# A hybrid state-space, attention and Hyena backbone: four reordered seams, and the carried part scaled on ScalarE

## The reference

```python
mod = silu(c) @ w_ada[l] + b_ada[l]; mod_c = silu(c_ctx) @ w_ada[l] + b_ada[l]
shift, scale, gate = jnp.split(mod[:, None, :], 3, axis=-1)
u = _layer_norm(h) * (1.0 + scale) + shift
uc = _layer_norm(hc) * (1.0 + scale_c) + shift_c
z, xbc, dtr, q, k, v, gd, hp, gh = jnp.split(u @ w_in, IN_SPLITS, axis=-1)

# state-space group: 4 groups of 4 heads of 64, state 128, chunks of 128 tokens, both directions
la = jnp.cumsum(dtc * a, axis=2)
y_diag = jnp.einsum('bclsgr,bcsgrp->bclgrp', w.astype(x.dtype), xc)
def step(h, inp):
    dec, st = inp
    return h * dec[..., None, None] + st, h
y_off = jnp.einsum('bclgn,bcgrpn->bclgrp', cc, h_start) * jnp.exp(la)[..., None]
y = y_f + flip(y_b) + dsk * xs
o_ssd = _rms_norm(y_ssd * silu(z)) * ssd_norm_w

# attention group: 4 heads, two score maps of 64 each
s = jnp.einsum('bqhmd,bkhmd->bhmqk', q, k) * DIFF_SCALE
p = softmax(s); attn = p[:, :, 0] - lam * p[:, :, 1]
o_diff = (_rms_norm(attn @ v) * (1.0 - lam_init)) * silu(gd)

# Hyena group: z = x1 * longconv(v); o_hy = x2 * longconv(z) * silu(gh), by FFT with implicit filters
h_new = _layer_norm(ALPHA * h + gate * (concat(o_ssd, o_diff, o_hy) @ w_out)) * ln_g + ln_b
```

## Time and profile before

| | us |
|---|---|
| median of 3 runs (lowest, highest) | 3764.7 (3757.56, 3769.51) |
| the profiled execution, its time | 3763.57 |
| its span in the trace | 3761.8 |
| granted TensorE clock, mean | 0.958 |
| busy: PE, DVE, ACT, POOL | 3348.2, 2404.3, 1104.9, 994.6 |
| state-space stages, about | 1487 to 1708 and 3335 to 3540 |
| norm stages, about | 4 to 91 and 2015 to 2103 |

### The profile page before, as it was taken

How to read it: one execution, slowest core, us unless ns; L and a number is a source line. 1 busy time by engine, 2 the same in 40 slices (tenths; PEclk the granted TensorE clock), 3 DMA queues, 4 the chain that set the end, 5 groups by cost and what they waited for, 6 DMA issues and landing times. The chain is left out here.

```text
span 3761.8 us, 47984 instructions
## 1 busy us (share of the span) xinstructions
PE 3348.2 (89%) x18164; PEld 2728.6 (73%) x18164; DVE 2404.3 (64%) x3965; ACT 1104.9 (29%) x2003; POOL 994.6 (26%) x790
## 2 busy tenths in 40 slices
PE   6999999999958887996997989999999588868798
PEld 2787888888848876665783677888888488845577
DVE  4134566765448996996665324556875489969755
ACT  3112222212335555332210311222221355523321
POOL 0033334342202222211220023433343022232111
PEclk9999999999979998998998999999999799989899
DMA  5354232223171331434426155322332633133441
GB/s 204 79 158 147 82 93 90 92 85 103 57 216 43 98 102 60 161 117 154 140 79 229 54 128 171 97 87 82 108 97 75 205 93 96 43 114 114 142 147 62
DMA packets 416681, 423.57 MB, mean 113 GB/s; under 512 B 57168, under 2 KB 353104, under 8 KB 415298
## 3 DMA queue, kind: packets, MB, share of 16 engines
q1 hardware_dynamic: 369316, 314.17, 28.8%
q10 hardware_dynamic: 47136, 106.32, 8.0%
HBM read 287.76 MB, written 124.01 MB: 109 GB/s over the span
## 5 line engine op out<-in xcount | busy, mean ns | idle before, releaser
L778 PE MATMUL l_p_acc<-l_u_hi,l_w_hi 128*128 128x512 f32 (+1 forms) x2208 | 606.0, 376 | 29.8 <-ACT l_p_stg L842 16.1
L778 PE MATMUL l_p_acc<-l_u_hi,l_w_lo 128*128 128x512 f32 (+1 forms) x2208 | 588.3, 368 | 0.0
L778 PE MATMUL l_p_acc<-l_u_lo,l_w_hi 128*128 128x512 f32 (+1 forms) x2208 | 587.1, 367 | 0.0
L778 PEld LDWEIGHTS l_p_acc<-l_u_hi,l_w_hi 128*128 128x128 f32 x2208 | 383.7, 189 | 106.8 <-issue 33.2
L693 POOL TENSOR_TENSOR l_w_hi<-l_wt,l_p_zero 128x1024 fp32r<-128x1024 f32 x100 | 199.3, 1993 | 925.1 <-PE l_p_acc L778 758.1
L778 PEld LDWEIGHTS l_p_acc<-l_u_hi,l_w_lo 128*128 128x128 f32 x2208 | 381.2, 189 | 71.9
L778 PEld LDWEIGHTS l_p_acc<-l_u_lo,l_w_hi 128*128 128x128 f32 x2208 | 381.3, 189 | 71.7
L1512 PE MATMUL l_at_pS<-l_at_k_hi,l_at_q 128*128 128x512 f32 (+1 forms) x400 | 166.0, 415 | 125.1 <-ACT l_at_prob L1628 68.9
L1753 DVE TENSOR_REDUCE l_at_nmax<-l_at_pS 128x1 f32<-128x1280 f32 (+1 forms) x144 | 197.4, 1371 | 121.0 <-PE l_at_pS L1513 119.1
L695 POOL TENSOR_TENSOR l_w_lo<-l_wt,l_w_hi 128x1024 fp32r<-128x1024 f32 x100 | 266.4, 2664 | 7.9
L935 DVE TENSOR_TENSOR l_p_R<-l_p_sw,l_p_rs 128x512 f32<-128x512 f32 x72 | 49.7, 690 | 286.4 <-PE l_p_sw L757 286.4
(11 more groups left out here) (362 smaller groups left out, 7193.2 us busy)
## 6 DMA issues: line engine op xcount, KB each, us to landing
l_wt<-w_in SPq DMA_DIRECT2D x104, 512.0 KB, 3.9
l_n_wa<-w_ada SPq DMA_DIRECT2D x10, 2048.0 KB, 17.0
kf_d<-l_p_R SPq DMA_DIRECT2D x72, 256.0 KB, 3.7
xbc_d<-l_p_fin ACTq DMA_DIRECT2D x28, 640.0 KB, 3.0
l_at_K<-kf_d SPq DMA_DIRECT2D x64, 256.0 KB, 3.1
qk_d<-l_p_late ACTq DMA_DIRECT2D x12, 1280.0 KB, 4.6
l_oT<-o_d SPq DMA_DIRECT2D x10, 1024.0 KB, 6.7
l_sd_fed<-xbc_d SPq DMA_DIRECT2D x72, 128.0 KB, 2.2
```

Source lines behind the costliest of these rows:

```text
L778: mm = pe.matmul(acc[:, a:a + w], (w_hi, w_lo)[wp][m % 2][:, k], (u_hi, u_lo)[up][:, k, t0 + c:t0 + c + w], start=(k == n == 0), stop=(k = ...
```

## The change

Four places. (1) In norm_stage VectorE's modulation(3) follows modulation(2) at once; the third batch's statistics and normalising are woven into the items behind, and modulation(5) comes after item 20. (2) In project_stage the last two of the eight gate tiles for z are moved to the end of the list. (3) In attention, head 0's queries are loaded in two parts, 256 latent columns first, the rest on SP behind the wait for the scores' inputs; TensorE waits for that rest at unit 2. (4) In ssd_stage the scaling of pU moves from one VectorE instruction of 128x512 to eight ScalarE passes of 128x64, each with its factor per partition; VectorE keeps the addition. `carried` now waits for ScalarE's semaphore (u_split).

```diff
@@ norm_stage, VectorE
-                statistics(0)
+                rows(0)
                 modulation(0)
                 modulation(1)
-                statistics(1)
+                rows(1)
                 modulation(2)
-                statistics(2)
                 modulation(3)
                 dve.wait_ge(modT_mm, 1)
                 dve.tensor_copy(modT[:].rearrange("p a b -> p (a b)"), pT[:, 0:4 * KD]).then_inc(modT_ready, 1)
                 dve.wait_ge(modT_ready, 1)
-                remainders(0)
-                remainders(1)
-                modulation(4)
-                remainders(2)
-                modulation(5)
+                last = batches[2]
+                dve.wait_ge(h_in[2], 16)
+                for n in range(KD):
+                    remainder(n)
+                    half_sums(last[n // 2], n % 2)
+                variances(2)
+                remainder(KD)
+                inverses(2)
+                for i, t in enumerate(last):
+                    remainder(KD + 1 + i)
+                    normalise(t)
+                modulation(FRONT)
+                for n in range(KD + 1 + len(last), len(items)):
+                    remainder(n)
+                    if n == gate_after[-1] + 2:
+                        modulation(FRONT + 1)
@@ norm_stage, ScalarE
                 for n in range(len(items)):
                     turned(n)
+                    if n == KD:
+                        deviation(2)
@@ attention_hyena_stage
+        first_q = slice(CTX, CTX + 2 * P)
+        rest_q = [slice(CTX + 2 * P, T)] + ([slice(t0, CTX)] if t0 < CTX else [])
+        def load_rest(queue, m, part):
+            lo, at = AD * m, slice(AD * part, AD * (part + 1))
+            for cols in rest_q:
+                queue.dma_start(q_s[at, 0, m, cols].bitcast(F32), qk_d[part, lo:lo + AD, cols]).then_inc(q_rest_in, 16)
...
-            queue.dma_start(q_s[at, s, m, t0:].bitcast(F32), qk_d[part, lo:lo + AD, t0:]).then_inc(score_in[s][m], 16)
+            cols = slice(t0, T) if h else first_q
+            queue.dma_start(q_s[at, s, m, cols].bitcast(F32), qk_d[part, lo:lo + AD, cols]).then_inc(score_in[s][m], 16)
...
                 for m in range(2):
                     sp.wait_ge(score_in[0][m], 96)
+                for m in range(2):
+                    for part in range(2):
+                        load_rest(sp, m, part)
                 load_values(0)
...
+                    if n == 2 and m == 0:
+                        pe.wait_ge(q_rest_in, 64 * len(rest_q))
@@ ssd_stage, TensorE
                     if n:
-                        pe.wait_ge(u_scaled, n)
+                        pe.wait_ge(u_split, n)
@@ ssd_stage, ScalarE
+                def scale_carried(n):
+                    gr, i = divmod(n, NO)
+                    act.wait_ge(u_mm, n + 1)
+                    if i == 0:
+                        act.wait_ge(picked, gr + 1)
+                    if n >= 2:
+                        act.wait_ge(y_mm, n - 1)
+                    for d in range(2):
+                        for h in range(HPG):
+                            last = act.activation(us[:, n % 2, d, h], pU[:, (d * HPG + h) * HD:(d * HPG + h + 1) * HD], ACT.Copy, scale=mine[:, gr % 2, 2, outs[i], d, h:h + 1])
+                    last.then_inc(u_split, 1)
...
                     todo = preps(j) if g < GROUPS else []
+                    if 0 <= n - 1 < NO * GROUPS:
+                        scale_carried(n - 1)
                     if todo:
                         prep(g, todo[0])
@@ ssd_stage, VectorE
-                def scale_carried(n):
-                    gr, i = divmod(n, NO)
-                    dve.wait_ge(u_mm, n + 1)
-                    if n >= 2:
-                        dve.wait_ge(y_mm, n - 1)
-                    decay = mine[:, gr % 2, 2, outs[i]].rearrange("p d h -> p (d h)")
-                    dve.tensor_tensor(us[:, n % 2].rearrange("p d h e -> p (d h) e"), pU[:, :].rearrange("p (k e) -> p k e", e=HD),
-                                      decay.unsqueeze(2).to_broadcast([P, 2 * HPG, HD]), ALU.mult).then_inc(u_split, 1)
+                def add_carried(n):
                     dve.wait_ge(u_split, n + 1)
                     dve.tensor_tensor(us[:, n % 2, 0], us[:, n % 2, 0], us[:, n % 2, 1], ALU.add).then_inc(u_scaled, 1)
@@ hybrid_backbone
-                                   ("gate", GD0, 4, t0, gate_d, None), ("gate", Z0, 8, t0, gate_z, None), ("conv_silu", XBC0, 12, 0, xbc_d, 0), ("conv_silu", XBC0 + 12 * P, 4, t0, xbc_d[1536:2048], 12),
+                                   ("gate", GD0, 4, t0, gate_d, None), ("gate", Z0, 6, t0, gate_z, None), ("conv_silu", XBC0, 12, 0, xbc_d, 0), ("conv_silu", XBC0 + 12 * P, 4, t0, xbc_d[1536:2048], 12),
...
+                                  + [("gate", Z0 + 6 * P, 2, t0, gate_z[6 * P:], None)],
```

More of the change, by code:

```diff
@@ L230, in acts @@
             return sum(by_act(i) for i in range(n))
+        gate_after = [n for n in range(20) if n % 5 != 4]
         def affine(n):
@@ L297, in _, with deviation @@
                 act.activation(cond[:], cond[:], ACT.Silu).then_inc(cond_ready, 1)
-                for b, t in enumerate(batches):
+                def deviation(b):
+                    t = batches[b]
                     act.wait_ge(var_ready, b + 1)
                     act.activation(mv[:, 2, t[0]:t[-1] + 1], mv[:, 1, t[0]:t[-1] + 1], ACT.Sqrt).then_inc(std_ready, 1)
+                deviation(0)
+                deviation(1)
                 act.wait_ge(modT_ready, 1)
@@ L315, in _, with half_sums, variances @@
                 step = 0
-                def statistics(b):
+                def half_sums(t, i):
+                    dve.bn_stats(st[:, t, i], xn[:, t, i * BANK:(i + 1) * BANK]).then_inc(dve_step, 1)
+                def variances(b):
                     nonlocal step
[L319 to L322, removed]
                     for i, t in enumerate(batches[b]):
@@ L332, in statistics, with normalise, rows @@
                     dve.wait_ge(rstd_ready, b + 1)
+                def normalise(t):
+                    dve.tensor_scalar(xn[:, t], xn[:, t], mv[:, 0, t:t + 1], mv[:, 3, t:t + 1], ALU.subtract, ALU.mult).then_inc(xn_ready, 1)
+                def rows(b):
+                    dve.wait_ge(h_in[b], 16)
                     for t in batches[b]:
-                        dve.tensor_scalar(xn[:, t], xn[:, t], mv[:, 0, t:t + 1], mv[:, 3, t:t + 1], ALU.subtract, ALU.mult).then_inc(xn_ready, 1)
+                        for i in range(2):
+                            half_sums(t, i)
+                    variances(b)
+                    inverses(b)
+                    for t in batches[b]:
+                        normalise(t)
                 def modulation(j):
@@ L340, in modulation, with remainder @@
                                              1.0 if 2 <= j < 4 else 0.0, ba[:, j % 2], ALU.add, ALU.add).then_inc(mod_ready, 1)
[L342 to L352, removed]
-                statistics(0)
+                def remainder(n):
+                    b, k = items[n]
+                    dve.wait_ge(hi_ready, n + 1)
+                    if by_act(n):
+                        dve.wait_ge(u_act, acts(n) + 1)
+                    else:
+                        scale, shift = affine(n)
+                        dve.tensor_scalar(u[:, n % 4, 0:width(b)], x_of(n), scale, shift, ALU.mult, ALU.add).then_inc(u_dve, 1)
+                        dve.wait_ge(u_dve, n - acts(n) + 1)
+                    dve.tensor_tensor(u_lo[:, k, cols(b)], u[:, n % 4, 0:width(b)], u_hi[:, k, cols(b)], ALU.subtract).then_inc(lo_ready, 1)
+                rows(0)
                 modulation(0)
                 modulation(1)
-                statistics(1)
+                rows(1)
                 modulation(2)
-                statistics(2)
                 modulation(3)
@@ L2217, in _ @@
                         weights(n)
[L2218 removed]
+                        add_carried(n)
                     if g < GROUPS:
```

10 lines of the change are left out of this document (6 added, 4 removed).

## The result

The changed kernel takes 3768.9 us (median of 20 runs, 3760.6 to 3784.97) against 3761.36 before (20 runs); the ratio is 1.0021, interval [1.0011, 1.0031]. It is slower, by some 8 us, where I forecast 27. The profiled execution has a span of 3769.2 us, 7.4 more than before's.

What follows compares the result with a forecast made beforehand. Mid state-space stage of layer 0, TensorE and VectorE are all but full, but four kinds of tick have different chains. Terms 49.9 − 14 − 5.4 − 3.1 = +27.4, that is 3791 us; range 3764 to 3814.

Steps and rivals of the forecast that it cites:

- the state-space sum: State-space stages of both layers: eight ScalarE passes lengthen the ticks, layer 0 +27.9 us, layer 1 +22.0, together +49.9.
- the projection's stalls: Projection stage: moving two tiles also moves woven filter work, where TensorE stalls 4.7 and 5.2 us; charged +1 us.
- Price of the passes: State-space stage: a 64-column ScalarE pass costs 315 ns, pitch .22 us, eight end 1.86 us after the first began.
- Rivals 1, 2 and 3: State-space passes: 1, pitch .125, 3757 us, chance .08; 2, ScalarE outside every chain, 3729, .04; 3, pitch .315, 3828, .09.
- rival 5: Norm, seam and attention edits bring nothing, since later waits swallow them: kernel 3813 us, chance .08.
- I move the whole rest by 1.43, to 6.77: State-space ticks with preparations: ScalarE's first copy begins 1.43 us later and all behind it follows, tick 5.34 to 6.77.
- my −.8 and −1.0: State-space stage, other ticks of the first three groups: us saved per group, −.8 in layer 0, −1.0 in layer 1.
- The drain of +1.2 a layer: End of each layer's state-space stage: one more set of passes, +1.2 us.
- Rival 4: State-space chain with preparations has unseen slack, so a delay of 1.43 us comes out as half: kernel 3773, chance .13.
- The seam: Projection's end in layer 0: a gate as last tile lets the next stage begin near 1050.85, −5.8 us.
- the part behind the turned vector: Norm stage after pT: shorter slow stretch, .5 us a layer charged for weaving, early store of the last modulation −2.4.
- the second chunk's turn: Attention's first loads: queries moved ahead of the second chunk u; bounds a 6.1 us gain and a loss of 1, half taken.

Runs made afterwards that it cites:

- the handover alone: The kernel before, tiles in the old order, with the planner's handover forced to 2.0 in layer 0 where it took 2.5: ratio 0.9979, −8 us.

## Why the prediction was off

The direction was right and the measured time lies in the range, near its lower end, but the change is +8 us, not +27. Two steps failed: the size of the state-space sum, 12 us too high, and the projection's stalls, charged at +1 and measured at about −8. By terms, each measured alone:

| term | forecast | measured |
|---|---|---|
| state-space | +49.9 | +38 |
| norm | −14 | −11 |
| projection | −5.4 | −14 |
| attention | −3.1 | −1.5 (0 within its interval) |

- **Price of the passes:** right. 330 ns each against 315, .20 apart against .22, eight in 1.75 against 1.86. The loop of the last group came out at 4.44 against 4.55. By the Trainium skill, ScalarE: Activation LUTs (What ACT_TABLE_LOAD costs), I had worked out an estimate of 332 ns a pass, which was better than my slope; the estimate's pitch of 239 ns was further off than mine (200 measured), and its sum, 6 us above mine, was further from the result. Rivals 1, 2 and 3, with pitches of .125, near nothing and .315, fall; rival 5, with nothing from the other three edits, falls by their −29.
- **What a late copy costs:** the step "I move the whole rest by 1.43, to 6.77" was right in mechanism and too large: the copy was 1.26 late and the tick 1.22 longer. In layer 1 the second tick of a group grew by 1.2, not 2.1, and the three after by .66, not .87. On the other side VectorE's relief was worth more than my −.8 and −1.0: all the ticks without preparations in the first three groups went to 4.44, and the last one before a new group fell from 5.32 to 4.86 in layer 0 and from 7.83 to 7.37 in layer 1. A group grew by about 5.0 in layer 0 and 3.8 in layer 1, where I had 6.3 and 5.1. The drain of +1.2 a layer is not seen. That is the 12 us. Rival 4, which had the chain give way by half, falls too: of 1.26 us of delay 1.22 reached the next pU. That the measured time is near its 3773 is chance.
- **The projection's stalls:** "I charge +1, between −4 and +8" was the step that came out beyond its own bounds. The seam was right: 5.9 us against 5.8. I wrote that the woven filter work moves and named the two waits of 4.7 and 5.2 us, but did not follow where the new plan puts the work that they wait for. The one at 879 went, the waits for transforms fell from 9.9 to 4.3 us, and the handover alone measured −8.
- **Norm:** the load behind the 2 MB transfer ended the wait, at 49.59 against 49.8 forecast. What failed is the part behind the turned vector. That vector began 3.1 and 4.7 us sooner after its stage's start (forecast 2.7 and 3.9), and the rest of the stage gave 1.1 and 1.8 more, where I had 2.9 and 4.1. Layer 1's terms as I wrote them add up to −8.0, not −8.4.
- **Attention:** the gain at the first scores of layer 0 (2.7 against 3.5 forecast) was gone again at the second chunk's turn, for which I had a loss as a bound. What the whole edit is worth the runs do not resolve.

## What to carry to other kernels

Moving an operation off a full engine pays only in the stretches where that engine ends the wait; the same move in the chain of another stretch costs nearly its whole length, so choose by stretch. Here one wide instruction with a broadcast factor became eight narrow ones with a factor per partition (.69 us became 1.75), and it was mostly their number that was paid. When tiles of a planned schedule are moved, compare the two plans' waits first: the plan's change can be worth as much as the move.

## What the runs showed that I had not expected

TensorE's waits in an unchanged stage came and went between executions of the same code (6.2 us on ScalarE's copies), which is more than half of what the norm edit gave. And one wait of about 5 us of TensorE in the projection was followed by a stretch at half clock (mean .91 over 20 us). That is worth little: .09 of 20 us makes an estimate of 1.8 us, and the run in which that wait is gone has the same mean granted clock over the stage, .99.
